# Three of ten weight remainders behind the convolution's norm go from GpSimd to VectorE

## The chip, the core and the metric

The kernel runs on one core of a Trainium2 chip. The metric is the device time of one launch in microseconds (us). Before the change it is 1906.09 us, the median of three runs (1905.41 to 1906.23).

## What is computed

The reference is two transformer-like blocks over 256 tokens of width 2048, in float32. What matters here is the middle of the second block, the convolution module:

```python
def conformer_conv(h, w_pw1, b_pw1, w_dw, b_dw, ln_g, ln_b, w_pw2, b_pw2):
    u = h @ w_pw1 + b_pw1
    a, gate = jnp.split(u, 2, axis=-1)
    u = a * jax.nn.sigmoid(gate)
    u = lax.conv_general_dilated(u, w_dw[:, None, :], ...) + b_dw
    u = jax.nn.silu(layer_norm_2(u, ln_g, ln_b))
    return u @ w_pw2 + b_pw2
```

The last line is the second projection, `w_pw2`, a 2048 x 2048 matrix. It follows the layer norm at once. Behind it come a residual, an rms norm and an MLP with a hidden width of 8192.

## The kernel before

**How a product is made.** TensorE multiplies in the type fp32r, which keeps fewer bits than float32. So each operand is split in two: a high part, which is the value rounded to fp32r, and a low part, which is what the rounding left over. A product is high x high, plus high x low, plus low x high. The activations stay on the chip with both parts (`pair.hi`, `pair.lo`). The weights are streamed: each chunk is a 128 x 1024 tile of float32, 512 KB, and there are 686 of them (`NC`), numbered by `c` in the order in which TensorE takes them. That order is laid down by hand in `plan()`.

**The life of a chunk.** SyncE loads it into one of seven buffers (`raw`) as soon as TensorE is through with the chunk seven before it (`sync`, line 605). ScalarE makes the high part with a copy into one of four buffers `wh` (`high`, line 738); it waits for the load and for TensorE to be through with the chunk four before (`s_mm`). Then VectorE (`low` in `vector`, line 1139) or GpSimd (`low` in `gpsimd`, line 669) subtracts the high part from the raw one, in place, and so makes the low part `wl`. Which of the two does it is set by the set `ON_POOL`: a chunk in it is GpSimd's, any other VectorE's. TensorE waits for the count of low parts of the engine in charge (`low_there`, `LOW_V`, `LOW_G`).

**Order on an engine.** Every engine runs its instructions strictly in the order in which its loop over `c` issues them. In the loops of ScalarE, VectorE and GpSimd the step `c` asks for the parts of chunk `c + 3` and then does the step's own work. What a step waits for holds up all that stands behind it on that engine.

**The stretch of the change.** The first chunk of the second projection is number `P1_END = LN2 = 398`. It is called +0 here, the next +1, and so on. Chunks +0 to +7 are the stage `p2g`: the first four output tiles of the projection together, with all 16 slices of the input, two slices to a chunk. It is written so because the slices of the input come out of the norm one after another. In chunks +0 to +2 the high parts of a slice are used first, and its low part after them (lines 2180, 2181, 2196). From chunk +3 on, each slice takes four pairs of a 512-wide matmul (line 2185) and a 256-wide one (line 2187), so a chunk is eight pairs. TensorE waits for a chunk's low part **ahead of the whole chunk**: in `chunk(c)` every stage of kind `G` but `bxg` calls `low_there(c)` first. From chunk +8 on the projection goes tile by tile, two chunks each (`high_products`, line 2036; `low_products`, line 2047), and there the low part is waited for only ahead of the low products. Chunk +8 is the tile 4, and its PSUM bank is that of tile 0: TensorE may start it only when VectorE has taken tile 0 out of the bank (lines 1309 and 1312, `bank_free`).

**The norm and VectorE's place in it.** `norm_conv()` of VectorE is issued whole at step `c = LN2`: means (lines 1810 to 1818), then for nine groups of slices (`NORMED`: two of one slice, seven of two) the subtraction of the mean (line 1828), the scaling (line 1843) and the low part of the activations (line 1834). Between them ScalarE makes the SiLU (line 1006) and the high part of the activations (line 1009), and from the fourth group on also one high part of the weights behind each group (line 738). The low part of chunk +6 would be asked for at step `LN2 + 3`, that of +8 at `LN2 + 5`, that of +10 at `LN2 + 7`: all three behind `norm_conv()`, and all three ahead of tile 0's evacuation, which stands at step `LN2 + 8`. ScalarE's share of that evacuation begins with a table load (line 859) and the high part of the sum (line 861); VectorE's low part of it is line 1315.

GpSimd's loop has nothing in this stretch but its low parts.

Of the kernel before, what the change touches and what calls it, by code (L numbers as in the profile page):

```python
# [211 lines left out]
def end(stage, t):  # L212
    return AT[stage, t].end


def first(stage, t=0):
    return next(c for c in range(NC) if STEP[c][0] is AT[stage, t])


P1, P1_END = first("p1g"), end("cv", 15)  # L220
# [7 lines left out]
PLAIN = {c for c in range(NC) if STEP[c][0].kind == "C"}  # L228
LOW_FIRST = set()
for _c in range(1, NC):  # L230
    _j, _i = STEP[_c]
    if _j.kind == "W" and _i > 0 and STEP[_c - 1][0].kind == "W" and _c - 1 not in LOW_FIRST:
        LOW_FIRST.add(_c)
ON_POOL = set(range(P1 + 2, P1_END + 12)) - set(range(P1_END, P1_END + 2)) - PLAIN

LOW_V, LOW_G, HIGH = {}, {}, {}
for _c in range(NC):
    HIGH[_c] = HIGH.get(_c - 1, 0) + (_c not in PLAIN)
    LOW_V[_c] = LOW_V.get(_c - 1, 0) + (_c not in ON_POOL and _c not in PLAIN)
    LOW_G[_c] = LOW_G.get(_c - 1, 0) + (_c in ON_POOL)  # L240

# [116 lines left out]
def _build(nc, a, out, ctx):  # L358
# [299 lines left out]
    def gpsimd(e):  # L658
        w = Waits(e)

        def low(c):
            if c not in ON_POOL:
                return
            w.wait_ge(s_hi, HIGH[c])
            if c >= P1 + 2:
                w.wait_ge(s_rstd, 4)
            if c >= P1_END + 2:
                w.wait_ge(s_wide, 4)
            e.tensor_tensor(wl[:, c % RAW, :], raw[:, c % RAW, :], wh[:, c % WN, :].bitcast(F32),  # L669
                            ALU.subtract).then_inc(s_low_g, 1)  # L670
# [461 lines left out]
    def vector(e):  # L1132
        w = Waits(e)

        def low(c):
            if c in ON_POOL or c in PLAIN:
                return
            w.wait_ge(s_hi, HIGH[c])
            e.tensor_tensor(wl[:, c % RAW, :], raw[:, c % RAW, :], wh[:, c % WN, :].bitcast(F32),  # L1139
                            ALU.subtract).then_inc(s_low_v, 1)  # L1140
# [847 lines left out]
    def tensor(e):  # L1988
# [10 lines left out]
        def low_there(c):  # L1999
            if c in ON_POOL:  # L2000
                w.wait_ge(s_low_g, LOW_G[c])
            else:
                w.wait_ge(s_low_v, LOW_V[c])
# [528 lines left out]
```

## Time and profile before

| | us |
|---|---|
| median of 3 runs (lowest, highest) | 1906.09 (1905.41, 1906.23) |
| the profiled execution | 1905.72 |
| its span, first to last instruction | 1903.7 |
| what lies around the span | 2.0 |
| TensorE busy | 1879.1 (99% of the span) |
| VectorE busy | 1488.1 (78%) |
| ScalarE busy | 961.4 (51%) |
| GpSimd busy | 412.3 (22%) |

The page calls TensorE's matmuls PE and its weight loads PEld, VectorE DVE, ScalarE ACT, GpSimd POOL and SyncE SP. Matmuls are pipelined: the page models an end for each that lies behind the start of the next, so the distance from start to start tells the pace, and an idle time shown is a little shorter than the gap in the stream. A row of the timeline gives the start in us from the span's start, the length in us, the engine, the line, what is written from what, how many instructions are merged in the row, and in brackets how long the engine had been idle before and who released it. GB/s and DMA shares play no part below.

### The profile page before, as it was taken

What the parts mean: (1) busy time and instruction counts of PE and PEld (TensorE: products, weight loads), DVE (VectorE), ACT (ScalarE), POOL (GpSimd) and SP (SyncE); (2) the same over time, 40 slices, a digit from 0 to 9 for tenths busy, and PEclk for the clock granted to TensorE, in tenths of its full rate; (3) what the DMA queues carried; (4) which work ended last, traced back from release to release, by engine and by line L of the source; (5) the groups of instructions that cost most, each with busy time, mean ns of one, the idle gap of its engine ahead of it and who ended that gap; (6) DMA issues with size and microseconds to landing.
All of it is one profiled execution on the core that took longest, in us unless ns stands there. A gap on an engine that the chain in (4) does not pass through costs nothing.

```text
span 1903.7 us, 28439 instructions
## 1 busy us (share of the span) xinstructions
PE 1879.1 (99%) x11210; PEld 1676.6 (88%) x11210; DVE 1488.1 (78%) x2235; ACT 961.4 (51%) x1346; POOL 412.3 (22%) x310
## 2 busy tenths in 40 slices
PE   9999999999999999999999999999999999999998
PEld 8989898888878788889899988998899889989987
DVE  7977899878899986779899996777567557656755
ACT  6655554434444445548654466554345445444544
POOL 0000344424366630000397744000000000000000
PEclk9999999999999999999999999999999999999999
DMA  9766666555656666676566656666666666666664
GB/s 333 250 193 192 192 199 180 174 165 179 192 176 185 180 187 197 200 231 199 161 197 218 200 176 189 200 209 200 204 204 199 202 205 201 200 204 204 200 202 153
DMA packets 105973, 377.45 MB, mean 198 GB/s; under 512 B 11888, under 2 KB 14448, under 8 KB 105712
## 3 DMA queue, kind: packets, MB, share of 16 engines
q1 hardware_dynamic: 105552, 375.10, 64.4%
q8 instruction: 89, 1.46, 0.3%
q10 hardware_dynamic: 288, 0.53, 0.1%
q14 instruction: 44, 0.36, 0.1%
HBM read 372.90 MB, written 2.69 MB: 197 GB/s over the span
## 4 chain that ended last, share of the span: by engine, by line
PE 73%; DVE 20%; issue 3%; ACT 2%; DMA 1%; POOL 0%; DVEq 0%; SPq 0%; ACTq 0%
PE bank L2036 24%; PE bank L2047 12%; PE bank L2103 7%; PE bank L2101 7%; PE bank L2102 7%; DVE bank L1757 6%; DVE wl L1139 5%; PE bank L2084 3%; PE bank L2086 3%; PE bank L2085 3%; ACT wh L738 2%; DMA raw<-in_w_bxg 1%; DVE wsc L1524 1%; PE bank L2180 1%; DVE upad L1294 1%
## 5 line engine op out<-in xcount | busy, mean ns | idle before, releaser
L1139 DVE TENSOR_TENSOR wl<-raw,wh 128x1024 fp32r<-128x1024 f32 x608 | 761.0, 1257 | 319.2 <-ACT wh L738 313.7
L738 ACT ACTIVATE wh<-raw 128x1024 fp32r<-128x1024 f32 x680 | 711.0, 1053 | 542.1 <-PE bank L2103 204.9
L2036 PE MATMUL bank<-Hr,wh 128*128 128x512 f32 x1536 | 351.3, 380 | 0.5 <-DVE scrB L1188 0.5
L2036 PEld LDWEIGHTS bank<-Hr,wh 128*128 128x128 f32 x1536 | 282.4, 189 | 36.9 <-issue 0.7
L669 POOL TENSOR_TENSOR wl<-raw,wh 128x1024 fp32r<-128x1024 f32 x72 | 172.7, 2415 | 292.3 <-DVE small L1713 234.1
L2101 PE MATMUL bank<-wh,Yr 128*128 128x512 f32 x560 | 212.3, 379 | 0.0
L2102 PE MATMUL bank<-wl,Yr 128*128 128x512 f32 x560 | 212.2, 379 | 0.0
L2103 PE MATMUL bank<-wh,Yr 128*128 128x512 f32 x560 | 212.2, 379 | 0.0
L2036 PE MATMUL bank<-Yr,wh 128*128 128x512 f32 x832 | 191.3, 380 | 1.5 <-ACT wh L738 0.6
L2047 PEld LDWEIGHTS bank<-Hr,wl 128*128 128x128 f32 x1536 | 187.0, 192 | 6.3 <-issue 1.1
L2047 PE MATMUL bank<-Hr,wl 128*128 128x256 f32 x1536 | 188.3, 275 | 0.0
L2036 PEld LDWEIGHTS bank<-Yr,wh 128*128 128x128 f32 x832 | 152.8, 189 | 21.7 <-issue 0.9
L2084 PE MATMUL bank<-wh,Hr 128*128 128x512 f32 x384 | 149.3, 389 | 4.5 <-DVE wl L1139 4.5
L2085 PE MATMUL bank<-wl,Hr 128*128 128x512 f32 x384 | 145.5, 379 | 0.0
L2086 PE MATMUL bank<-wh,Hr 128*128 128x512 f32 x384 | 145.5, 379 | 0.0
L2118 PE MATMUL bank<-Hr,wh 128*128 128x256 f32 x448 | 123.9, 276 | 1.3 <-POOL wl L669 1.1
L1757 DVE SCALAR_TENSOR_TENSOR bank<-upad,cst,bank 128x256 f32<-128x256 f32 x290 | 121.7, 480 | 2.3
L2119 PE MATMUL bank<-Hr,wh 128*128 128x256 f32 x448 | 123.2, 275 | 0.0
L2120 PE MATMUL bank<-Hr,wl 128*128 128x256 f32 x448 | 123.2, 275 | 0.0
L2101 PEld LDWEIGHTS bank<-wh,Yr 128*128 128x128 f32 x560 | 105.8, 189 | 15.0
L2102 PEld LDWEIGHTS bank<-wl,Yr 128*128 128x128 f32 x560 | 105.8, 189 | 15.0
L2103 PEld LDWEIGHTS bank<-wh,Yr 128*128 128x128 f32 x560 | 105.8, 189 | 15.0
(380 smaller groups left out, 2740.2 us busy)
## 6 DMA issues: line engine op xcount, KB each, us to landing
raw<-in_w_up SPq DMA_DIRECT2D x128, 512.0 KB, 4.2
raw<-in_w_dn SPq DMA_DIRECT2D x128, 512.0 KB, 4.2
raw<-in_w_g SPq DMA_DIRECT2D x96, 512.0 KB, 3.6
raw<-in_w_p SPq DMA_DIRECT2D x80, 512.0 KB, 3.8
raw<-in_w_b SPq DMA_DIRECT2D x48, 512.0 KB, 3.6
raw<-in_w_out SPq DMA_DIRECT2D x32, 512.0 KB, 3.6
raw<-in_w_q SPq DMA_DIRECT2D x16, 512.0 KB, 4.3
raw<-in_w_av SPq DMA_DIRECT2D x16, 512.0 KB, 4.2
```

What stands on the lines that cost most here:

```text
L669: e.tensor_tensor(wl[:, c % RAW, :], raw[:, c % RAW, :], wh[:, c % WN, :].bitcast(F32), ALU.subtract).then_inc(s_low_g, 1)
L738: e.activation(wh[:, c % WN, :], raw[:, c % RAW, :], ACT.Copy).then_inc(s_hi, 1)
L1139: e.tensor_tensor(wl[:, c % RAW, :], raw[:, c % RAW, :], wh[:, c % WN, :].bitcast(F32), ALU.subtract).then_inc(s_low_v, 1)
L1757: e.scalar_tensor_tensor(ac, pad[:, j:j + T], wj, ac, ALU.mult, ALU.add).then_inc(s_v, w.own())
L2036: ins = e.matmul(dst, wh[:, s, kk * 128:kk * 128 + 128], by_turns(pair.both[:, :, k, :]), start=i == 0 and kk == 0, stop=i == j.nch - 1 an ...
L2047: ins = e.matmul(dst, wl[:, r, kk * 128:kk * 128 + 128], in_turns(pair.hi[:, k, :]), start=False, stop=i == j.nch - 1 and kk == 7, skip_gr ...
L2084: e.matmul(dst, xh, rh, start=first_part and kk == 0, stop=False)
L2085: e.matmul(dst, xh, rl, start=False, stop=False)
L2086: ins = e.matmul(dst, xl, rh, start=False, stop=last_part and kk == 1)
L2101: e.matmul(dst, xh, rh, start=first_part and kk == 0, stop=False)
L2102: e.matmul(dst, xh, rl, start=False, stop=False)
L2103: ins = e.matmul(dst, xl, rh, start=False, stop=last_part and kk == 1)
```

## The change

The set of chunks whose low part is GpSimd's is written differently. Behind the norm it held +2 to +11, ten chunks. Now it holds +2 to +5 and +7, +9, +11, seven chunks. +6, +8 and +10 fall to VectorE. Nothing else in the kernel differs: the order of steps, the loads, the high parts and the matmuls are the same, and the counts `LOW_V` and `LOW_G` follow from the set. Ahead of the norm, from `P1 + 2` to `P1_END`, the set is what it was.

```diff
@@ -231,7 +231,8 @@
     _j, _i = STEP[_c]
     if _j.kind == "W" and _i > 0 and STEP[_c - 1][0].kind == "W" and _c - 1 not in LOW_FIRST:
         LOW_FIRST.add(_c)
-ON_POOL = set(range(P1 + 2, P1_END + 12)) - set(range(P1_END, P1_END + 2)) - PLAIN
+ON_POOL = set(range(P1 + 2, P1_END)) | set(range(P1_END + 2, P1_END + 6)) | set(range(P1_END + 7, P1_END + 12, 2))
+ON_POOL -= PLAIN
 
 LOW_V, LOW_G, HIGH = {}, {}, {}
 for _c in range(NC):
```

## Rows read from the trace of the kernel before

**Rows 1.** The page: busy time and share of the span of each engine.
```profile
PE 1879.1 (99%) x11210; PEld 1676.6 (88%) x11210; DVE 1488.1 (78%) x2235; ACT 961.4 (51%) x1346; POOL 412.3 (22%) x310
```

**Rows 2.** Whom TensorE waited for: us in total, times, the longest.
```profile
PE bank L2084 <- DVE wl L1139: 5.7, 11, 1.5
...
PE bank L2118 <- POOL wl L669: 1.1, 1, 1.1
...
PE bank L2036 <- ACT wh L738: 0.6, 1, 0.6
```

**Rows 3.** Timeline of TensorE around the second projection: start, length, line, idle before.
```profile
1142.56 0.35 PE L2180 MATMUL bank<-Yr,wh 128*128 128x256 f32 x1
1142.74 0.28 PE L2181 MATMUL bank<-Yr,wl 128*128 128x256 f32 x1
...
1148.04 0.38 PE L2185 MATMUL bank<-Yr,wh 128*128 128x512 f32 x1
...
1155.90 0.38 PE L2185 MATMUL bank<-Yr,wh 128*128 128x512 f32 x1
...
1161.03 0.27 PE L2187 MATMUL bank<-Yr,wl 128*128 128x256 f32 x1
1161.35 1.99 PE L2036 MATMUL bank<-Yr,wh 128*128 128x512 f32 x8
1163.18 1.95 PE L2047 MATMUL bank<-Yr,wl 128*128 128x256 f32 x16
...
1168.42 1.95 PE L2047 MATMUL bank<-Yr,wl 128*128 128x256 f32 x16
1170.20 1.89 PE L2036 MATMUL bank<-Yr,wh 128*128 128x512 f32 x8
1172.66 1.97 PE L2036 MATMUL bank<-Yr,wh 128*128 128x512 f32 x8 [0.56 <-ACT wh L738]
```

**Rows 4.** Timeline of GpSimd behind the norm (ten low parts in all).
```profile
1138.00 4.71 POOL L669 TENSOR_TENSOR wl<-raw,wh 128x1024 fp32r<-128x1024 f32 x2 [18.49 <-PE bank L2330]
1145.01 17.34 POOL L669 TENSOR_TENSOR wl<-raw,wh 128x1024 fp32r<-128x1024 f32 x7 [2.30 <-ACT wh L738]
1162.53 2.37 POOL L669 TENSOR_TENSOR wl<-raw,wh 128x1024 fp32r<-128x1024 f32 x1 [0.18 <-ACT wh L738]
```

**Rows 5.** Timeline of VectorE, the end of the norm and the first evacuations.
```profile
1156.64 0.69 DVE L1834 TENSOR_TENSOR Yr<-bank,Yr 128x512 fp32r<-128x512 f32 x1 [1.84 <-ACT Yr L1009]
1160.36 0.48 DVE L1309 SCALAR_TENSOR_TENSOR Xf<-bank,cst,Xf 128x256 f32<-128x256 f32 x1 [3.02 <-PE bank L2187]
1160.88 0.42 DVE L1312 TENSOR_TENSOR Xf<-Xf,bank 128x256 f32<-128x256 f32 x1
1164.31 0.87 DVE L1315 SCALAR_TENSOR_TENSOR Hr<-Xf,cst,Hr 128x256 fp32r<-128x256 f32 x1 [3.01 <-ACT Hr L861]
```

**Rows 6.** Line 1139 from 1131 to 1175 us: lengths in ns, shortest, median, longest.
```profile
L1139 DVE TENSOR_TENSOR wl<-raw,wh x4: 1214/1218/1226, 1133.0 to 1173.7; 128x1024 fp32r<-128x1024 f32 x4
```

**Rows 7.** Timeline of ScalarE, the end of the norm and what follows.
```profile
1156.50 1.05 ACT L738 ACTIVATE wh<-raw 128x1024 fp32r<-128x1024 f32 x1
1158.78 1.06 ACT L738 ACTIVATE wh<-raw 128x1024 fp32r<-128x1024 f32 x1 [1.23 <-PE bank L2187]
1161.40 1.06 ACT L738 ACTIVATE wh<-raw 128x1024 fp32r<-128x1024 f32 x1 [1.56 <-PE bank L2187]
1163.77 0.51 ACT L861 ACTIVATE Hr<-Xf,cst 128x256 fp32r<-128x256 f32 x1
1171.48 1.99 ACT L738 ACTIVATE wh<-raw 128x1024 fp32r<-128x1024 f32 x2
```

**Rows 8.** Timeline near 961 to 973 us: one form of VectorE instruction, GpSimd idle or busy.
```profile
960.67 0.43 DVE L1294 SCALAR_TENSOR_TENSOR upad<-scrB,scrB 128x256 f32<-128x256 f32 x1 [0.31 <-ACT scrB L846]
970.93 2.08 DVE L1294 SCALAR_TENSOR_TENSOR upad<-scrB,scrB 128x256 f32<-128x256 f32 x1 [0.32 <-ACT scrB L846]
970.36 4.91 POOL L669 TENSOR_TENSOR wl<-raw,wh 128x1024 fp32r<-128x1024 f32 x2
```

**Rows 9.** The program's end: last matmul, then busy times and granted clock (after POOL).
```profile
1895.74 0.38 PE L2140 MATMUL bank<-wh,Yr 128*128 128x512 f32 x1
...
1896.12:1898.38 2.26, 0.00 (x1) 0.00 (x0) 1.07 (x3) 1.24 (x4) 0.00 (x0) 1.00 0.67 268
1899.00:1903.70 4.70, 0.00 (x0) 0.00 (x0) 0.31 (x1) 0.31 (x1) 0.00 (x0) 0.50 0.56 223
```

**Rows 10.** The first matmuls (timeline), then their busy time (how many touch it) by half microseconds.
```profile
1.12 4.52 PE L2335 MATMUL bank<-ones 128*128 128x128 f32 x26 [1.12 <-DVE ones L1851]
...
3.50:4.00 0.50, 0.50 (x4) 1.00 0.88 340
4.00:4.50 0.50, 0.50 (x7) 1.00 0.99 406
```

## The prediction

> **What bounds the kernel.** I read the busy shares first: TensorE is busy for 99% of the span and GpSimd for 22% [rows 1]. So a low part can gain time only where TensorE waits for it. The view of waits says where it did: in the whole program TensorE waited for a low part of GpSimd once, for 1.1 us, and at line 2118, the first projection, not the second [rows 2]. Then I read the timelines of the four engines through the second projection. TensorE's shows a stream: chunk +3 begins at 1148.04, and 40 pairs of a 512-wide and a 256-wide matmul run to the start at 1161.03 plus 0.11 us, so 1161.14 [rows 3]. That is 13.10 us for five chunks, 2.62 us each. Chunk +6 begins at 1155.90, and no wait stands before it. GpSimd makes its ten low parts at about 2.4 us each: two from 1138.00, seven from 1145.01 to 1162.35 and one to 1164.90 [rows 4]. The seven are +4 to +10, one each 2.48 us. So +6 was ready at 1145.01 + 3 x 2.48 = 1152.4, 3.5 us before its chunk; +8 at 1157.4, with its low products in the row of 1163.18; +10 at 1162.4, with its low products in that of 1168.42 [rows 3, 4]. All three are early. There is nothing to gain here, and the question is what VectorE's place in its own queue costs.
>
> **The change, part by part.** *GpSimd loses three instructions*, 3 x 2.4 us. Nothing waited for them and nothing is queued behind them but other low parts, so this is worth nothing. It holds whatever GpSimd does: its remaining parts +7, +9 and +11 follow ScalarE's high parts as before, and each was ready over 3 us ahead of its use.
>
> *VectorE gains three instructions* of 1.22 us [rows 6]. They are no faster for TensorE unless VectorE reaches them in time, and each is queued behind the one before, so I take them in order.
>
> *The low part of +6.* It stands behind the whole norm. The norm's last instruction on VectorE starts at 1156.64 and ends at 1157.33; it had itself waited for ScalarE [rows 5]. Instructions of VectorE follow one another 0.08 us before the modelled end, so the low part starts at 1157.25 and ends at 1158.47. The high part that it needs was long there. TensorE restarts 0.05 us behind a VectorE instruction that it waits for (line 1312 ends at 1161.30, line 2036 starts at 1161.35 [rows 3, 5]), so at 1158.52. It wanted to start at 1155.90, and it waits ahead of the whole chunk, so no matmul of +6 goes ahead. **The stall is 2.62 us.** A first matmul behind an idle time takes 0.35 us where the next takes 0.28 [rows 3]: 0.07 us more. TensorE is now 2.69 us late.
>
> *Who is held up by that.* Everything that waits for TensorE shifts with it: SyncE's loads (a load is asked for six chunks ahead, some 15 us, so it is hidden), ScalarE's high parts of +10 and +11, which started 0.26 us behind the end of +6 and +7 [rows 7], and the evacuation of tile 0. Nothing that TensorE does later gets shorter.
>
> *The low part of +8.* It is VectorE's next. It ends by 1162.1 even if it stands behind one of GpSimd's; its low products now come at 1163.18 + 2.69 = 1165.9. It costs nothing, and is covered by 3.8 us.
>
> *The low part of +10.* Its high part waits for chunk +6, so it is made from 1158.78 + 2.69 = 1161.47 to 1162.53. The low part follows at 1162.55 and ends at 1163.77, and the evacuation of tile 0 is queued behind it. Tile 0 was ready for line 1309 at 1160.36, now at 1163.05 [rows 5]; it starts at 1163.69 instead, 0.64 us later. Chunk +8 needs tile 0's bank. Line 1312 ends 0.94 us after line 1309 starts, at 1164.63, so TensorE starts +8 at 1164.68. With the 2.69 us alone it would have been 1164.04: another 0.64 us.
>
> *Is the 0.64 us kept?* No. Further on TensorE waits for the high part of +12 until 1172.66 [rows 2, 3]. That comes at the end of a chain on ScalarE which starts with the high part of +11, released by the end of +7, and goes through a table load and four evacuations [rows 7]; it does not depend on tile 0 being out at 1161.30 rather than 1161.95, since ScalarE takes it up only at 1163.77. So this chain shifts by 2.69 us only, and the high part is there for a start at 1175.35. TensorE's stream before it ended at 1170.20 + 8 x 0.218 = 1171.94 (0.218 us from a 512-wide matmul to the next, 1.75 us for eight; each row's last matmul has its modelled end behind that). With 3.33 us it ends at 1175.27, in time. The 0.64 us goes into a wait that was there, and the sum stays **2.69 us**.
>
> *What VectorE's gain in work does to the rest.* The three cost 3.7 us of VectorE where it had been idle for 3.02 us ahead of line 1309 [rows 5]. That is why the evacuation moves. Behind the four evacuations VectorE's order is as before.
>
> **The sum.** 2.62 + 0.07 + 0.64 - 0.64 = 2.7 us. Against the profiled execution: a span of 1903.7 + 2.7 = 1906.4 and a time of 1905.72 + 2.7 = 1908.4. That execution stood 0.4 us below the median of the runs, so for the median I say 1906.09 + 2.7 = **1908.8 us**. This is 0.14%, below the 0.2% (3.8 us) which I take for the least that a measurement tells from no change.
>
> **The unknown cost: TensorE's clock.** No wait of TensorE in this trace is longer than 1.5 us [rows 2], so none shows what 2.6 us does. The nearest row is the program's end. The last matmul ends at 1896.12; the granted clock is 1.00 (2.4 GHz) for another 2.26 us and then 0.50 (1.2 GHz) [rows 9]. The new stall, counted in the same way from the modelled end at 1156.06 to 1158.52, is 2.46 us. This is longer by 0.2 us, so a fall is about as likely as not. Below: nothing, if the clock stays. Above: the first matmuls of the program, which start at 1.12, go at a slow pace until 4.0 and then nearly twice as fast [rows 10], though the record of the clock gives 1.00 for both. A stay of 2.9 us at half pace costs 1.4 us of work; were both +6 and +7 wholly slow, it would be 5.2 us. I take 1.4 us for a fall, because the first rows are the only stay at low pace with work in it. The Trainium skill, in the page "TensorE: Matmul & The Clock Gate", section "Why this matters for your kernels", advises against idle gaps longer than this one; by that advice the clock would hold here and the sum would stay 2.7 us, while the row at the end speaks for a fall.
>
> **The rivals.** *A: the stall lowers the clock* (slower by over 0.2%). Place: chunks +6 and +7. For it is the fall 2.26 us after the last matmul; against it that the end's idle time may have met the chip at another moment. It decides if a stall about as long as those 2.26 us is enough in mid-program. Price 1.4 us, total 4.1 us, 1910.2; with up to 1.7 us 1910.5.
>
> *B: the low part of +6 has to wait for GpSimd.* Line 1294, which reads two operands from SBUF, takes 0.43 us with GpSimd idle and 2.08 us when it starts inside one of GpSimd's low parts [rows 8]; line 1315 took 0.87 us in the same way [rows 4, 5]. The low part is of that kind. It starts at 1157.25, and GpSimd's next one (+9) can start only behind the high part that ends at 1157.55 [rows 7], so VectorE is first by 0.3 us. If GpSimd came first, the low part would start at about 1160.0 and TensorE at 1161.3: 5.4 us of stall, 1911.6 without a fall of the clock. The Trainium skill ("SBUF — State Buffer", the part on the shared port pair) says that whoever starts first holds the pair for its whole instruction and that the other blocks; rows 8 agree. By that rule, too, the order decides, and it gives the same two sums.
>
> *C: no stall* (faster or equal). VectorE would have to make +6 in one of its idle times before 1155.90 or GpSimd's relief would have to shorten the norm. The code's order excludes the first. Against the second: the norm's VectorE instructions read one operand from PSUM, and at its end VectorE waits for ScalarE (1.84 us) [rows 5]. The gain could be no more than the 0.56 us wait of rows 3: 1905.5 to 1906.1.
>
> **Chances.** The forecast (2.7 us, the clock holds) 0.48; A 0.43; B 0.05; C 0.04, half of it faster. So faster 0.02, within 0.2% 0.50, slower 0.48. The range runs from 1908.1 (a stall half a microsecond shorter, and the runs' own scatter) to 1910.9 (A with its upper price and that scatter); B and C are left out.
>
> **What would show it.** Right: 611 low parts on VectorE and 69 on GpSimd; a new row in which line 2185 waits for line 1139, about 2.5 us; the low part of +6 from about 1157.3; the gap ahead of +8 at about 0.8 us in place of 0.2; the wait of 0.56 us before 1172.66 gone or nearly so. For A: a granted clock below 1.00 around 1158 to 1162, and pairs at twice 0.33 us. Wrong: no wait at line 2185, or a low part of 2 us or more there (B), or all later rows shifted by another amount than the stall.

## The result, and the profile after

The changed kernel takes **1910.01 us** (median of 16 runs, 1908.30 to 1910.74); the kernel before takes 1905.86 us beside it (16 runs, 1905.32 to 1906.59). The ratio is 1.002, with a 95% interval of 1.0013 to 1.0027. The change costs 4.2 us. The interval leaves 1 out, and 4.2 us is a little more than the 3.8 us that the prediction took for the least to be told from no change.

The 16 times are not one group. Six lie between 1908.30 and 1909.06, with a middle of 1908.6. Ten lie between 1909.89 and 1910.74, with a middle of 1910.3. Nothing lies between. Against 1905.86 the first group is 2.7 us slower, the second 4.4 us. The same kernel has two outcomes, and the profiled execution (1910.32 us, span 1908.3) is of the second. The line numbers are one higher than before.

The busy times, as the page has them (TensorE, its weight loads, VectorE, ScalarE, GpSimd); compare [rows 1]:

```profile
PE 1882.0 (99%) x11210; PEld 1678.9 (88%) x11210; DVE 1492.5 (78%) x2238; ACT 961.1 (50%) x1346; POOL 405.7 (21%) x307
```

Three instructions have gone from GpSimd to VectorE, and nothing else has changed in number: line 1140 runs 611 times and line 670 runs 69 times, as forecast. The view of waits around the second projection (1140 to 1180 us: who waited for whom, us in total, times, the longest):

```profile
PEld bank L2186 <- DVE wl L1140: 2.7, 1, 2.7
...
PE bank L2186 <- DVE wl L1140: 2.5, 1, 2.5
...
PE bank L2037 <- DVE Xf L1313: 0.4, 1, 0.4
...
PE bank L2037 <- ACT wh L739: 0.2, 1, 0.2
```

The first two rows are one wait, seen by the weight load and by the matmul: TensorE waits once for a low part of VectorE. It is the longest wait of TensorE in the program [rows 2]. TensorE's timeline, to hold beside [rows 3]; line 2186 is the 512-wide matmul of a pair:

```profile
1155.85 0.38 PE L2186 MATMUL bank<-Yr,wh 128*128 128x512 f32 x1
1156.06 0.27 PE L2188 MATMUL bank<-Yr,wl 128*128 128x256 f32 x1
1158.79 0.48 PE L2186 MATMUL bank<-Yr,wh 128*128 128x512 f32 x1 [2.45 <-DVE wl L1140]
1159.11 0.27 PE L2188 MATMUL bank<-Yr,wl 128*128 128x256 f32 x1
...
1160.32 0.63 PE L2186 MATMUL bank<-Yr,wh 128*128 128x512 f32 x1
1160.75 0.42 PE L2188 MATMUL bank<-Yr,wl 128*128 128x256 f32 x1
1160.96 0.63 PE L2186 MATMUL bank<-Yr,wh 128*128 128x512 f32 x1
...
1165.68 0.27 PE L2188 MATMUL bank<-Yr,wl 128*128 128x256 f32 x1
1166.40 1.99 PE L2037 MATMUL bank<-Yr,wh 128*128 128x512 f32 x8 [0.45 <-DVE Xf L1313]
...
1177.32 1.97 PE L2037 MATMUL bank<-Yr,wh 128*128 128x512 f32 x8 [0.17 <-ACT wh L739]
```

Chunk +5 ends at 1156.06 + 0.11 = 1156.17, and +6 starts at 1158.79: a gap of 2.62 us. Behind it the first pairs take 0.33 us, then a pair takes 0.64 us (1160.32 to 1160.96). The windows view says what happened in between (stretch, length, then busy time and instructions of TensorE, its loads, VectorE, ScalarE and GpSimd, then the granted clock):

```profile
1156.44:1158.79 2.35, 0.00 (x1) 0.01 (x1) 1.88 (x3) 1.38 (x2) 0.89 (x1) 1.00 0.67 178
1158.79:1160.05 1.26, 1.26 (x7) 1.18 (x8) 1.26 (x1) 0.00 (x0) 1.26 (x1) 1.00 0.32 130
1160.05:1163.46 3.41, 3.41 (x12) 2.89 (x12) 1.98 (x1) 0.28 (x1) 0.90 (x1) 0.50 0.00 0
1163.46:1166.40 2.94, 2.50 (x16) 2.04 (x14) 2.04 (x3) 1.13 (x2) 0.00 (x0) 1.00 0.52 178
```

The clock fell to 0.50 (1.2 GHz) 1.26 us **after TensorE had started again**, stayed there for 3.41 us of full work and came back. Half of that is 1.7 us lost. This is the one execution of the changed kernel with a timeline, and it is of the upper group. That the other nine of that group had such a fall, and the six of the lower none, is read from their times. The mean granted clock of each run fits: 0.998 in seven of the ten and 0.999 in all six (3.41 us at half pace take 0.0009 off the mean of the run, so that rounding hides it in some).

VectorE and GpSimd, to compare with [rows 4, 5]:

```profile
1156.91 0.69 DVE L1835 TENSOR_TENSOR Yr<-bank,Yr 128x512 fp32r<-128x512 f32 x1 [1.83 <-ACT Yr L1010]
1157.52 4.51 DVE L1140 TENSOR_TENSOR wl<-raw,wh 128x1024 fp32r<-128x1024 f32 x2
1164.27 1.23 DVE L1140 TENSOR_TENSOR wl<-raw,wh 128x1024 fp32r<-128x1024 f32 x1 [2.24 <-ACT wh L739]
1165.41 0.48 DVE L1310 SCALAR_TENSOR_TENSOR Xf<-bank,cst,Xf 128x256 f32<-128x256 f32 x1
...
1152.85 2.39 POOL L670 TENSOR_TENSOR wl<-raw,wh 128x1024 fp32r<-128x1024 f32 x1 [2.65 <-ACT wh L739]
1157.90 3.05 POOL L670 TENSOR_TENSOR wl<-raw,wh 128x1024 fp32r<-128x1024 f32 x1 [2.66 <-ACT wh L739]
```

The low part of +6 is issued at the norm's heels, at 1157.52. VectorE's two in a row take 4.51 us instead of 2.4, and GpSimd's of +9 takes 3.05 instead of 2.4: they wait for each other.

The account of this execution against the one before, in gaps and stretches of TensorE: the stall 2.62; chunks +6 and +7 from 1158.79 to 1165.79, 7.00 us instead of 5.24, so 1.76 (0.10 for the first matmul's restart and 1.66 for the clock); the gap ahead of +8 0.61 instead of 0.21, so 0.40; and from +8 to the start of +12 10.92 instead of 11.31, so -0.39. The sum is 4.39 us. (Chunk +7 alone took 2.91 us, from 1162.88, instead of 2.62: the clock was still low at its head. This matters for the gap ahead of +8, below.) Another 0.27 us lay between the executions before the stretch began (1156.17 against 1155.90). The spans differ by 4.6 us.

### The profile page after: what moved, and what is told of

The parts are those of the page before. It is cut to its first block, busy times and chain, and to the rows that moved or that the text cites. A ratio compares the mean times of both kernels' runs of the same rounds, so it can differ in the third digit from the quotient of the medians.

```text
span 1908.3 us, 28439 instructions
## 1 busy us (share of the span) xinstructions
PE 1882.0 (99%) x11210; PEld 1678.9 (88%) x11210; DVE 1492.5 (78%) x2238; ACT 961.1 (50%) x1346; POOL 405.7 (21%) x307
## 4 chain that ended last, share of the span: by engine, by line
PE 76%; DVE 17%; issue 3%; ACT 3%; DMA 1%; POOL 0%; DVEq 0%; ACTq 0%
PE bank L2037 24%; PE bank L2048 12%; PE bank L2103 7%; PE bank L2104 7%; PE bank L2102 7%; DVE wl L1140 5%; DVE bank L1758 3%; PE bank L2085 3%; PE bank L2087 3%; PE bank L2086 3%; ACT wh L739 2%; PE bank L2119 1%; PE bank L2120 1%; PE bank L2121 1%; DMA raw<-in_w_bxg 1%
## 5 line engine op out<-in xcount | busy, mean ns | idle before, releaser
L670 POOL TENSOR_TENSOR wl<-raw,wh 128x1024 fp32r<-128x1024 f32 x69 | 166.1, 2423 | 303.2 <-DVE small L1714 234.1
```

## The experiments

The changed kernel's row is the one from above (16 runs, beside 1905.86 us for the kernel before). The others are medians of 11 runs each. The kernels "+6 early, +10 back", "stall half filled" and "high part of +12 early" stood beside 1906.04 us for the kernel before, the other four beside 1906.02 us.

| kernel | low parts on VectorE | us | lowest, highest |
|---|---|---|---|
| changed | +6, +8, +10 | 1910.01 | 1908.30, 1910.74 |
| only +6 | +6 | 1910.28 | 1908.37, 1910.62 |
| only +8 and +10 | +8, +10 | 1906.47 | 1905.79, 1906.97 |
| +6 issued early | +6, +8, +10 | 1906.40 | 1905.88, 1907.16 |
| +6 early, +10 back | +6, +8 | 1906.28 | 1905.96, 1906.36 |
| stall filled | +6, +8, +10 | 1908.64 | 1908.19, 1909.07 |
| stall half filled | +6, +8, +10 | 1908.62 | 1908.29, 1909.01 |
| high part of +12 early | none | 1905.19 | 1904.88, 1905.50 |

### One part of the change alone: only +6

```diff
-ON_POOL = set(range(P1 + 2, P1_END)) | set(range(P1_END + 2, P1_END + 6)) | set(range(P1_END + 7, P1_END + 12, 2))
+ON_POOL = set(range(P1 + 2, P1_END)) | (set(range(P1_END + 2, P1_END + 12)) - {P1_END + 6})
```

> Only the low part of chunk +6 goes to VectorE; +8 and +10 stay GpSimd's. Theory (the whole loss is the wait for +6, and the fall of the clock behind it): the stall of 2.6 us ahead of chunk +6 and, in most executions, the slow clock behind it stay as in the changed kernel; tile 0's evacuation is not held up, so the gap ahead of chunk +8 is 0.2 us and the wait for ScalarE's high part of +12 is back at about 0.6 us; the time is the changed kernel's, 1908.5 without and 1910.2 with the fall. Rival (each of the three moved low parts costs its share): a third of the loss, about 1907.2.

Measured: 1910.28 us, and again two groups, five runs at 1908.37 to 1909.00 and six at 1910.28 to 1910.62. One of the three moved low parts makes the whole loss. TensorE's timeline has the stall and, ahead of chunk +12, the old wait of 0.6 us:

```profile
1158.77 0.73 PE L2186 MATMUL bank<-Yr,wh 128*128 128x512 f32 x1 [2.54 <-DVE wl L1140]
1165.99 1.99 PE L2037 MATMUL bank<-Yr,wh 128*128 128x512 f32 x8
...
1177.32 1.97 PE L2037 MATMUL bank<-Yr,wh 128*128 128x512 f32 x8 [0.58 <-ACT wh L739]
```

This profiled execution is of the upper group too, and its windows show the fall at another moment than above:

```profile
1156.40:1158.70 2.30, 0.00 (x0) 0.00 (x0) 1.91 (x2) 1.30 (x2) 2.15 (x2) 1.00 0.66 187
1158.80:1160.00 1.20, 1.20 (x4) 1.02 (x5) 0.00 (x0) 0.00 (x0) 1.20 (x1) 0.53 0.23 92
1160.00:1163.00 3.00, 3.00 (x13) 2.67 (x12) 0.00 (x0) 0.00 (x0) 0.92 (x1) 0.62 0.00 0
1163.00:1165.00 2.00, 2.00 (x13) 1.83 (x13) 0.01 (x1) 1.06 (x1) 0.45 (x1) 1.00 0.37 74
```

The clock was still 1.00 in the idle time. A mean of 0.53 over the 1.20 us from 1158.80 puts the fall at 1158.87, only 0.10 us behind TensorE's restart, and a mean of 0.62 over the next 3.00 us puts its end at 1162.28. That is again 3.41 us at half pace, and +6 and +7 together took 7.01 us, as in the changed kernel (7.00).

### The other part alone: only +8 and +10

```diff
-ON_POOL = set(range(P1 + 2, P1_END)) | set(range(P1_END + 2, P1_END + 6)) | set(range(P1_END + 7, P1_END + 12, 2))
+ON_POOL = set(range(P1 + 2, P1_END)) | (set(range(P1_END + 2, P1_END + 12)) - {P1_END + 8, P1_END + 10})
```

> Only the low parts of +8 and +10 go to VectorE; +6 stays GpSimd's. Theory: no stall at chunk +6 and no fall of the clock; tile 0's evacuation starts about 0.6 us late behind the low part of +10, chunk +8 starts 0.6 us late, and the wait for the high part of +12 takes that up: 1905.9, no difference from the kernel before. Rival 1 (the 0.6 us is kept): 1906.5. Rival 2 (each moved part costs its share): about 1908.6.

Measured: 1906.47 us, 0.45 us above the kernel before. The stall and the fall are gone, as the theory says, but the time is rival 1's. VectorE and GpSimd in this run, and TensorE ahead of chunk +8:

```profile
1157.68 1.22 DVE L1140 TENSOR_TENSOR wl<-raw,wh 128x1024 fp32r<-128x1024 f32 x1
1160.32 1.90 DVE L1140 TENSOR_TENSOR wl<-raw,wh 128x1024 fp32r<-128x1024 f32 x1 [1.42 <-ACT wh L739]
1162.14 0.47 DVE L1310 SCALAR_TENSOR_TENSOR Xf<-bank,cst,Xf 128x256 f32<-128x256 f32 x1
...
1158.07 3.07 POOL L670 TENSOR_TENSOR wl<-raw,wh 128x1024 fp32r<-128x1024 f32 x1 [2.67 <-ACT wh L739]
...
1163.12 1.99 PE L2037 MATMUL bank<-Yr,wh 128*128 128x512 f32 x8 [1.37 <-DVE Xf L1313]
```

The low part of +10 takes 1.90 us, and GpSimd's part of +9 is under way until 1161.14; that one took 3.07 us, and VectorE's part of +8 was there first. I read this as each waiting for the other. So tile 0 comes out of its bank 1.3 us late, not 0.6, and the wait that should take it up holds only 0.7. What is over is kept: 0.6 us by these rows, 0.45 by the medians. In the change itself this is hidden: the stall puts 2.6 us between +8 and +10.

### The same work, another place in the queue: +6 issued inside the norm

```diff
                 if n >= 1:
                     low_part(n - 1)
+                if n == 6:
+                    low(LN2 + 6)
             low_part(len(NORMED) - 1)
...
-            if c + 3 < NC and c not in (POST, LAST_PAD, LN2 - 2):
+            if c + 3 < NC and c not in (POST, LAST_PAD, LN2 - 2, LN2 + 3):
                 low(c + 3)
```

> The changed kernel, but VectorE issues the low part of +6 inside the norm, behind the sixth of the nine low parts of the activations, where ScalarE's high part of +6 has just been made. Theory (the place in VectorE's queue costs, not the engine): the low part runs from about 1150.0 to 1151.2, the stall and the fall are gone, and the norm's last groups come in time: 1905.9. Rival (VectorE is too full behind the norm, whatever the order): the norm's low parts of the activations come later by 1.2 us and TensorE waits for them instead, 1906.5 to 1907.1.

Measured: 1906.40 us, 0.4 us above before and 3.6 us below the changed kernel, with one group of times. VectorE makes the same three low parts as in the change.

```profile
1150.37 1.23 DVE L1140 TENSOR_TENSOR wl<-raw,wh 128x1024 fp32r<-128x1024 f32 x1 [0.25 <-ACT wh L739]
...
1156.99 0.69 DVE L1835 TENSOR_TENSOR Yr<-bank,Yr 128x512 fp32r<-128x512 f32 x1 [1.83 <-ACT Yr L1010]
1157.59 1.22 DVE L1140 TENSOR_TENSOR wl<-raw,wh 128x1024 fp32r<-128x1024 f32 x1
1160.22 1.91 DVE L1140 TENSOR_TENSOR wl<-raw,wh 128x1024 fp32r<-128x1024 f32 x1 [1.42 <-ACT wh L739]
```

The norm's last instruction comes when it came before (its distance to the stretch's start is the same), though 1.2 us of work were put ahead of it: VectorE had idle time there, waiting for ScalarE. So the engine was not too full; its order was wrong for TensorE. The 0.4 us that remain look like those of the run with +8 and +10: line 1140 takes 1.91 us here and 1.90 us there, and TensorE waits 1.4 us ahead of +8 in both. From the end of +7 to the start of +12 TensorE takes 0.63 us longer than before.

### +6 early and +10 back on GpSimd

```diff
-ON_POOL = set(range(P1 + 2, P1_END)) | set(range(P1_END + 2, P1_END + 6)) | set(range(P1_END + 7, P1_END + 12, 2))
+ON_POOL = set(range(P1 + 2, P1_END)) | (set(range(P1_END + 2, P1_END + 12)) - {P1_END + 6, P1_END + 8})
```

> As the run with +6 issued inside the norm, but +10 is GpSimd's again (VectorE: +6 early and +8). Theory (what was left there, 0.4 us, is the low part of +10: it stands ahead of tile 0's evacuation and has to let GpSimd's +9 finish): tile 0 comes out of its bank at 1161.3 or a few tenths later, TensorE's wait of 1.4 us ahead of chunk +8 is gone, the wait for the high part of +12 is back at 0.6 us: 1906.0, no difference from before. Rival (the 0.4 us comes from the early +6 or from +8): 1906.4.

Measured: 1906.28 us, 0.24 us above before. The wait ahead of +8 is gone, as expected, but the other one has grown from 0.56 us to 0.88:

```profile
1157.94 7.74 POOL L670 TENSOR_TENSOR wl<-raw,wh 128x1024 fp32r<-128x1024 f32 x3 [2.65 <-ACT wh L739]
...
1164.61 1.34 DVE L1316 SCALAR_TENSOR_TENSOR Hr<-Xf,cst,Hr 128x256 fp32r<-128x256 f32 x1 [3.01 <-ACT Hr L862]
...
1173.45 1.97 PE L2039 MATMUL bank<-Yr,wh 128*128 128x512 f32 x8 [0.88 <-ACT wh L739]
```

VectorE's part of +8 pushes GpSimd's three back, the last of them runs until 1165.68, and the first instruction of VectorE that reads two operands from SBUF takes 1.34 us beside it. In the kernel before it took 0.87 us, also beside a part of GpSimd's [rows 4, 5]. It is on ScalarE's chain. From the end of +7 to the start of +12 TensorE takes 0.49 us longer than before, against 0.63 us with +10 on VectorE. The medians say the same: 0.24 us is left of 0.38. So the theory was right that the wait ahead of +8 goes, but wrong on the time: taking +10 back gave only 0.14 us, and 1906.28 is nearer to the rival's 1906.4 than to 1906.0. The larger share stays with +8, by way of GpSimd. These are differences of a few tenths, about as large as the scatter of the runs.

### The stall filled, wholly and by half

```diff
+            if c == LN2 + 6:
+                spare(10, 7)
             if c < NC - 4:
                 chunk(c)
```

> The changed kernel, with ten spare products of ones (20 matmuls in the trace, about 2.3 us, into an unused part of a PSUM bank) ahead of the wait for chunk +6. They leave the stall as it is and keep TensorE busy in it. Theory (1.7 us of the loss are the clock's fall): granted clock 1.00 throughout, pairs of chunk +6 at 0.33 us, all executions within half a microsecond around 1908.5, none near 1910.2. Rival (the second part of the loss has another cause, as the ports or a DMA): the time stays at 1908.3 to 1910.7 with a median near 1910.

Measured: 1908.64 us, all 11 runs within 0.9 us. TensorE's timeline and two windows:

```profile
1156.32 2.40 PE L2219 MATMUL bank<-ones 128*128 128x128 f32 x20
1158.92 0.48 PE L2186 MATMUL bank<-Yr,wh 128*128 128x512 f32 x1 [0.21 <-DVE wl L1140]
...
1156.00:1160.00 4.00, 3.79 (x30) 3.50 (x29) 2.95 (x3) 1.93 (x3) 1.96 (x1) 1.00 0.59 196
1160.00:1164.00 4.00, 4.00 (x27) 3.69 (x26) 3.18 (x2) 1.06 (x1) 1.09 (x1) 1.00 0.26 73
```

Chunk +6 starts as late as in the changed kernel, yet the upper group of times is gone and the granted clock is 1.00. So 2.6 us are the wait (1908.64 against 1906.02), and what the upper group has on top is the clock. Useless matmuls save 1.4 us of the median. With five spare products (`spare(5, 7)`):

> The changed kernel with five spare products (ten matmuls in the trace, about 1.2 us) at the head of the stall ahead of chunk +6; the idle time that is left is about 1.3 us. Theory (the clock falls for the idle time, and waits of that length left it alone elsewhere in the program): all executions near 1908.6, clock 1.00, as with ten. Rival (any hole in this place can lower the clock): part of the executions near 1910.3.

Measured: 1908.62 us, 1908.29 to 1909.01. TensorE's timeline, and its wait ahead of +8 from the view of waits:

```profile
1156.04 1.28 PE L2219 MATMUL bank<-ones 128*128 128x128 f32 x10
1158.65 0.48 PE L2186 MATMUL bank<-Yr,wh 128*128 128x512 f32 x1 [1.33 <-DVE wl L1140]
...
PE bank L2037 <- DVE Xf L1313: 0.7, 1, 0.7
```

An idle time of 1.33 us is left, the granted clock of the profiled execution is 1.00 from 1150 to 1170 us, and by the times it fell in none of 11 runs. Both traces also show the changed kernel's queue without a fall: the gap in TensorE's stream ahead of +8 is 0.86 us here (1163.99 to 1164.85) and 0.87 us with the stall wholly filled, against 0.21 before.

### A wait of the kernel before, taken away

The wait of 0.56 us ahead of chunk +12 belonged to the kernel before. ScalarE idles for 1.43 us between two evacuations, with the high part of +12 still to be made.

```diff
-            if c + 3 < NC and c + 3 not in HIGH_POST and c + 3 not in HIGH_LN and c not in (LN2 - 2, LN2 - 1, LN2):
+            if c + 3 < NC and c + 3 not in HIGH_POST and c + 3 not in HIGH_LN and c not in (LN2 - 2, LN2 - 1, LN2, LN2 + 9):
                 high(c + 3)
...
+                if t == 3:
+                    high(LN2 + 12)
                 w.wait_ge(s_comb, j.comb)
```

> The kernel before (all ten low parts on GpSimd); only ScalarE makes the high part of +12 ahead of its share of tile 3's evacuation instead of behind it, in an idle time of 1.4 us. Theory (the wait of 0.56 us ahead of chunk +12 is on TensorE's path and nothing takes its place): TensorE starts +12 at 1171.95 instead of 1172.66, 1905.3 us. Rival (tile 3 comes later and the next bank or chunk waits instead): 1906.0.

Measured: 1905.19 us against 1906.04; the slowest of its 11 runs (1905.50) is below the fastest of the 27 of the kernel before beside it (1905.67). Against that, the interval of the ratio, 0.9987 to 1.0004, holds 1, and three of the kernel before's 16 runs beside the change lie at 1905.32 to 1905.41. So the trace shows that the wait is gone, and a gain of 0.85 us is likely, not proven:

```profile
1169.25 1.04 ACT L738 ACTIVATE wh<-raw 128x1024 fp32r<-128x1024 f32 x1
1170.78 0.51 ACT L863 ACTIVATE Hr<-Xf,cst 128x256 fp32r<-128x256 f32 x1 [0.49 <-DVE Xf L1314]
...
1170.22 3.62 PE L2038 MATMUL bank<-Yr,wh 128*128 128x512 f32 x16
```

Sixteen matmuls stand in one row where there were eight, a wait and eight. The high part fits ahead of tile 3, whose evacuation comes when it came before (ScalarE's high part of the sum at 1170.78, before at 1170.76), and +12 starts at 1170.22 + 1.75 = 1171.97, as forecast (1171.95).

## Why the prediction held, point by point

**Nothing to gain on GpSimd.** Right: no wait for it was there to remove, and taking it off these three chunks shortened nothing.

**The low part of +6 and the stall.** Right in path and size: 2.62 us forecast, 2.62 us measured; VectorE issued it 0.61 us behind the start of the norm's last instruction, as worked out. The restart cost 0.10 us instead of 0.07. The run with +6 alone and the run with +6 early show that this is the cause, from both sides.

**The low part of +8.** Right for the path: its bound of 1162.1 was met (1162.03).

**The low part of +10 and tile 0.** Right in kind, and in size for the case that it was worked out for. Where the clock held (the stall filled wholly or by half), the gap ahead of +8 grew by 0.66 and 0.65 us, where 0.64 was forecast. In the profiled execution of the change it grew by 0.40 only. There the slow clock stretched +7 by 0.29 us, while the low part of +10, which is released by the end of +6, went on at its own pace; that accounts for the difference. The wait for +12 took all of the 0.40, as worked out. But the reason given was good for this change only. That GpSimd and VectorE wait for each other here was left out of this step, though it stood in rival B. Without the stall it comes to 1.3 us of delay, and in the run with +8 and +10 alone I expected no difference where 0.45 us was measured.

**The clock.** The forecast (the clock holds) and rival A (it falls) had nearly the same chance, 0.48 and 0.43. Both came: six of 16 runs are as forecast and ten as in A. So the median lies in A, 1.2 us above the number forecast, and inside the range only because the range was drawn out to A's upper price. The lower group, 1908.6, is 0.2 us from the 1908.8 forecast. The term that was off is the price of a fall: 1.4 us, from the first matmuls of the program, where 1.66 us was measured. The upper price of 1.7 us is close to that, but no row stood behind it, so that this is luck as far as the rows go.

What made A likely was a comparison: the stall, counted from the modelled end, is 2.45 us, and at the end of the program the clock had held for only 2.26 us [rows 9]. It gave the right outcome for most runs, but not the moment. In both traces with a fall the clock outlived the whole idle time (2.45 and 2.54 us) and fell behind the restart. Why it fell in ten runs and not in six is open; no trace of a run of the lower group was kept.

The Trainium skill ("TensorE: Matmul & The Clock Gate", "Why this matters for your kernels") advises against idle gaps longer than this one. By that advice the clock would have held, and in 10 of 16 runs, by their times, it did not: here the measurement decides.

**Rival B.** VectorE came first by 0.38 us (1157.52 against 1157.90), where 0.3 had been worked out. That the loser waits was seen on both engines. **Rival C** did not show.

## What to carry to other kernels

Read from the timeline when each product is needed and where its maker stands in its own queue: here the faster engine began 1.35 us after the product was needed and cost 2.6 us, where the slower one was 3.5 us early. When a new wait of TensorE is about as long as this one (2.5 us), price the clock with it, and be ready for two groups of times rather than one. Work moved between two engines that wait for each other, as VectorE and GpSimd do here, moves their other instructions too.

## What was not expected

- The clock fell **after** TensorE had resumed, not in the idle time: 1.26 us behind the restart in the trace of the change and 0.10 us behind it in that of the run with +6 alone. Both then show 0.50 for 3.41 us under full load.
- The outcome differs from run to run of one kernel: by the times, the idle time of 2.45 us met a fall in 10 of 16 runs (and that of 2.54 us in 6 of 11 with +6 alone), the 1.33 us in none of 11.
- VectorE's and GpSimd's subtractions, 1.22 and 2.38 us alone, took 1.90 and 3.07 us when they met, and the instruction of line 1316, 0.48 us where GpSimd is idle, took 1.34 us beside one of GpSimd's.
